# Two decoder layers with 32 routed experts on one core: fewer expert pairs scattered through DRAM, read back inside the expert stage, and a new router chain

## What is computed

```python
x = x + concat(rglru, conformer_conv, retention)(rmsnorm(x) @ w_in) @ w_out
x = x + hier_moe(rmsnorm(x), ...)

def hier_moe(x, wg, bg, we, be, w1, w3, w2):
    pg = softmax(x @ wg + bg); g = argmax(pg)              # 1 of 4 groups
    top_v, top_i = top_k((x @ we + be)[group g], 2)        # 2 of its 8 experts
    gates = pg[g] * softmax(top_v)
    y = sum over the 32 experts e: gates_e * (silu(x @ w1_e) * (x @ w3_e)) @ w2_e
```

## Time and profile before

| | us |
|---|---|
| median of three runs | 904.78 |
| profiled execution, its own time | 911.48 |
| its span, first to last instruction | 909.2 |
| TensorE busy (4940 matmul records) | 795.3 |
| VectorE busy | 352.5 |
| ScalarE busy | 169.7 |
| GpSimd busy | 119.1 |
| moved by DMA | 266.57 MB |

### The profile page before, as it was taken

One profiled execution on the slowest core, in us unless ns is written; L12 is line 12 of the kernel. 1 busy time (PEld: TensorE's weight loads), 2 busy tenths in 40 slices (PEclk: granted clock), 3 DMA queues, 4 the chain that ended last, 5 costly groups with the idle time before them and its releaser, 6 DMA issues.

```text
span 909.2 us, 12840 instructions
## 1 busy us (share of the span) xinstructions
PE 795.3 (87%) x4940; PEld 469.6 (52%) x4940; DVE 352.5 (39%) x865; ACT 169.7 (19%) x357; POOL 119.1 (13%) x163
## 2 busy tenths in 40 slices
PE   7999999979998887887789999999899987788784
PEld 6745554765554444454277446447655534445451
DVE  2468986532111111111722789955311211111127
ACT  2304113101211111111211121221011111111113
POOL 0101030030111010011000000300211101011010
PEclk9999999989999999999979999999999999999997
DMA  9961933879999999997983038348799999999961
GB/s 291 306 243 60 317 98 88 279 220 353 419 416 416 414 416 414 416 416 275 340 267 138 1 125 245 97 122 321 233 392 415 415 418 415 416 416 416 392 232 53
DMA packets 107918, 266.57 MB, mean 293 GB/s; under 512 B 34775, under 2 KB 68587, under 8 KB 90902
## 3 DMA queue, kind: packets, MB, share of 16 engines
q1 hardware_dynamic: 97898, 254.11, 75.2%
q0 software_dynamic: 8640, 9.11, 2.9%
q10 hardware_dynamic: 1340, 2.80, 0.8%
HBM read 262.85 MB, written 25.92 MB: 318 GB/s over the span
## 4 chain that ended last, share of the span: by engine, by line
PE 52%; DMA 24%; issue 12%; DVE 6%; SPq 3%; ACT 1%; POOL 1%; DVEq 0%; POOLq 0%; ACTq 0%
DMA ring<-in_moe_w 22%; PE psum L1008 13%; PE psum L723 12%; PE psum L1034 9%; PE psum L702 7%; PE psum L654 3%; PE psum L734 2%; SPq L509 1%; DVE arena L1649 1%; DMA rows<-xn_scratch,sg 1%; PE psum L892 1%; PE psum L660 1%; SPq L505 1%; SPq L501 1%; PE psum L790 1%
## 5 line engine op out<-in xcount | busy, mean ns | idle before, releaser
L1008 PE MATMUL psum<-ring,arena 128*64 128x256 f32 x1984 | 229.2, 383 | 36.1 <-DVE arena L1649 26.0
L1008 PEld LDWEIGHTS psum<-ring,arena 128*64 128x64 f32 x1984 | 148.5, 137 | 102.2 <-issue 38.5
L1034 PE MATMUL psum<-ring,arena 128*64 128x512 f32 x496 | 124.9, 633 | 39.3 <-DMA ring<-in_moe_w 31.2
L1657 DVE SCALAR_TENSOR_TENSOR arena<-arena,psum 128x128 f32<-128x128 f32 x64 | 18.1, 282 | 298.7 <-ACT arena L1945 283.1
L723 PE MATMUL psum<-ring,uT 128*128 128x512 f32 x256 | 113.0, 595 | 0.0
L1034 PEld LDWEIGHTS psum<-ring,arena 128*64 128x64 f32 x496 | 40.3, 144 | 107.5 <-issue 106.2
L1649 DVE TENSOR_TENSOR arena<-psum,gff 128x512 f32<-128x512 f32 x64 | 41.2, 685 | 118.9 <-PE psum L654 118.9
L2063 POOL DMA_INDIRECT y_scratch<-arena,sg x28 | 28.3, 1010 | 374.8 <-ACT arena L1930 314.0
L723 PEld LDWEIGHTS psum<-ring,uT 128*128 128x128 f32 x256 | 47.7, 190 | 55.3 <-issue 54.5
L1935 ACT ACTIVATE arena<-psum 128x256 f32<-128x256 f32 x62 | 23.8, 384 | 280.1 <-PE psum L1008 270.8
L1930 ACT ACTIVATE arena<-psum,sg 128x512 f32<-128x512 f32 x64 | 44.0, 687 | 129.3 <-PE psum L1034 129.3
(11 more groups left out here) (285 smaller groups left out, 656.0 us busy)
## 6 DMA issues: line engine op xcount, KB each, us to landing
ring<-in_moe_w SPq DMA_DIRECT2D x186, 1024.0 KB
ring<-in_w_in SPq DMA_DIRECT2D x24, 1024.0 KB
ring<-in_w_out SPq DMA_DIRECT2D x8, 1024.0 KB
y_scratch<-sg SPq DMA_DIRECT2D x2, 2304.0 KB
ring<-y_scratch SPq DMA_DIRECT2D x4, 1024.0 KB, 9.8
arena<-in_state_ret SPq DMA_DIRECT2D x16, 128.0 KB, 6.2
out<-arena SPq DMA_DIRECT2D x16, 128.0 KB, 2.6
xn_scratch<-rows ACTq DMA_DIRECT2D x4, 512.0 KB, 4.6
```

The source lines that it names most:

```text
L1008: i = pe.matmul(b[64 * j:64 * j + 64, 0:FE], xsT[:, u // 2, k, s], w[j][:, k, :], start=k == 0, stop=k == KT - 1, skip_group_check=True)
L1034: i = pe.matmul(b[64 * q:64 * q + 64, :], hT[:, q, f, :], w[:, 512 * j:512 * j + 512], start=f == 0, stop=f == 1, skip_group_check=True)
```

## The change

- **Way back.** Pairs 0 to 9 go through DRAM (`VIA_DRAM` = 10), pairs 10 to 15 by matmul. Each pair has its own sums now: five parts (`back0` to `back4`) that take turns in banks 6 and 7, each added to `x` by VectorE before the next may use the bank. GpSimd reads the rows of pairs 0 to 9 back by an indirect gather per tile and choice (`read_back`, two DMAs a tile, tiles in the order 1, 2, 0), issued at its turns 10, 11 and 12 behind the wait for the results of that pair; VectorE adds them (`sums`) at its turns 12, 13 and 14. A row that is not in `y_scratch` is skipped by the DMA, so VectorE clears both landing tiles first (`clear`).
- **No zeros.** `y_scratch` is filled once, from `w_out`, in the first layer's mixer, and never zeroed.
- **Spare.** It is expert 30 now, not 31; its w2 is loaded between the weights of the pairs (at SP's turn 4).
- **Input weights.** SP issues granules 6, 7, 0, 1, 8, 3, 4, 2, 5 of the next `w_in` right behind the last expert's w2, each when its granule is free, and 9 to 11 after the extra loop.
- **Router.** TensorE transposes raw `x`; the logits come out token by row and VectorE applies 1/rms and bias in one step; ScalarE scales and stores the rows. Slots are one-hot marks of the rank in the expert, made on VectorE; a first table gives the tokens (`tab`) and starts the gathers, a second the gates (`tabg`), a third the overflow (`tabo`), whose marks (`overs`) VectorE makes after the first tokens. `keep_clock` has 11, 5, 5 and 4 matmuls in place of 17, 26 and 17.
- **Turn.** `up` waits for x0 alone and for x1 half way; `tokens` is cut in two around `up` of the second expert.

```diff
-VIA_DRAM = NPAIR - 2
+VIA_DRAM = 10
+BY_MATMUL = NPAIR - VIA_DRAM
+READ_BACK = (1, 2, 0)
-WAIT_NORM, WAIT_CHOICE, WAIT_MARKS, WAIT_ROWS = (13, 8), 17, 26, 17
+WAIT_NORM, WAIT_CHOICE, WAIT_MARKS, WAIT_GATES, WAIT_ROWS = (13, 8), 11, 5, 5, 4
 # SP
-                sp.dma_start(y_dram.rearrange("(p r) (h n) -> p (r h) n", p=64, h=2),
-                             bc(sg[0:64, 2:3, :], [64, 2 * 9, 512])).then_inc(y_zeroed, 16)
+                    if p == 4:
+                        sp.wait_ge(idx_ready, l + 1)
+                        for f in range(2):
+                            sp.dma_start(spare_w2[f], w2[l, NE - 2, 128 * f:128 * f + 128, :]).then_inc(spare2_in, 16)
-                sp.wait_ge(scattered, 16 * VIA_DRAM * (l + 1))
-                for t, (o, n) in enumerate(TILES):
-                    sp.dma_start(ring[0:n, 9 + t, :] ...).then_inc(sums_in[t], 16)
+                if l + 1 < DEPTH:
+                    for g, use in zip((6, 7, 0, 1, 8, 3, 4, 2, 5), last_use):
+                        xfull(sp, *use, l)
+                        project_in(l + 1, g)
 # TensorE
+                def experts2_back(p):
+                    pair, it = pair_of(p)
+                    up(2 * pair, it, spare=p == NPAIR - 1)
+                    if p - 2 >= VIA_DRAM:
+                        give_back(p - 2, (2, 3))
+                        give_back(p - 2, (4,))
+                    down(1 - pair, it if pair else it - 1)
+                    turn_h(2 * pair, it)
+                    if p + 1 < NPAIR:
+                        tokens(pair + 1, it, (0,))
+                    up(2 * pair + 1, it)
+                    if p + 1 < NPAIR:
+                        tokens(pair + 1, it, (1,))
+                    turn_h(2 * pair + 1, it)
+                    if p - 1 >= VIA_DRAM:
+                        give_back(p - 1, (0, 1))
 # VectorE
+                def clear():
+                    own(dve.memset(again[0], 0.0))
+                    own(dve.memset(again[1], 0.0))
+                    own.wait()
+                    dve.sem_inc(again_clear, 1)
+                def experts2_back(p):
+                    pair, it = pair_of(p)
+                    if p - 2 >= VIA_DRAM:
+                        given_back(p - 2, (0, 1))
+                        if p - 2 - VIA_DRAM < 3:
+                            sums(p, READ_BACK[p - 2 - VIA_DRAM])
+                            if p - 2 - VIA_DRAM < 2:
+                                clear()
+                        given_back(p - 2, (2, 3, 4))
+                    if p - 1 >= VIA_DRAM:
+                        rest(p - 1, 0)
+                    hidden(2 * pair, it)
+                    if p - 1 >= VIA_DRAM:
+                        rest(p - 1, 1)
+                        low(p - 1)
+                    if p + 1 < NPAIR:
+                        tokens(pair + 1, it)
+                    hidden(2 * pair + 1, it)
 # GpSimd
+                def read_back(t):
+                    o, n = TILES[t]
+                    pool.wait_ge(again_ready, l + 1)
+                    pool.wait_ge(scattered, 16 * VIA_DRAM * (l + 1))
+                    pool.wait_ge(again_clear, 3 * l + READ_BACK.index(t) + 1)
+                    for k in range(2):
+                        pool.indirect_dma_start(out=again[k][0:n, :], out_offset=None, in_=y_dram, ...)
...
                     if g < VIA_DRAM:
                         scatter(g)
                     else:
-                        way_back(g - VIA_DRAM)
+                        way_back(g)
                     if g + 2 < NPAIR:
+                        if g >= VIA_DRAM:
+                            for j in range(2):
+                                xfreed(pool, f"y{j}", *pair_of(g), l)
                         gate_of(g + 2)
+                    if 0 <= g - VIA_DRAM < 3:
+                        read_back(READ_BACK[g - VIA_DRAM])
```

More of the change, by code:

```diff
@@ L415, in expert_job @@
             pair, e = 2 * it + u, 4 * it + u
-            b, n = {"x0": (0, pair), "x1": (1, pair), "h": (2, e), "hT": (3, e), "y0": (4, pair), "y1": (5, pair)}[kind]
+            back = 2 * it + u - VIA_DRAM
+            b, n = {"x0": (0, pair), "x1": (1, pair), "h": (2, e), "hT": (3, e), "y0": (4, pair), "y1": (5, pair),
+                    "back0": (6, 3 * back), "back1": (7, 2 * back), "back2": (6, 3 * back + 1), "back3": (7, 2 * back + 1),
+                    "back4": (6, 3 * back + 2)}[kind]
             return b, l * PER_BANK[b] + EXPERT_BASE[b] + n
[L419 to L429, removed]
         def xfull(eng, kind, u, it, l):
@@ L1031, in down @@
                                 w = ring[:, 6 * pair + 3 * q + 2, 1024 * f:1024 * f + 1024]
-                                if spare and q:
+                                if spare and not q:
                                     w = spare_w2[f]
@@ L1066, in experts2 @@
-                def experts2(pair, it, first=False):
+                    if 4 in parts:
+                        b = begin("back4", pair, it)
+                        for n_, y in enumerate((y_top, y_mid, y_low)):
+                            for q in range(4):
+                                i = pe.matmul(b[32 * q:32 * q + 32, 0:256], back[:, pair, SEQ:NT], y[:, 256 * q:256 * q + 256],
+                                              start=n_ == 0, stop=n_ == 2, skip_group_check=True)
+                        finish(i, "back4", pair)
+                        return
@@ L1082, in _ @@
                     experts2(1, it)
[L1083 to L1091 removed]
+                for p in range(VIA_DRAM, NPAIR):
+                    experts2_back(p)
+                give_back(NPAIR - 2, (2, 3))
@@ L1624, in _ @@
-                by_pair = tab[:, :, 0:NE].rearrange("p v (g i) -> p v g i", i=2)
-                for i in range(2):
-                    h = slice(64 * i, 64 * i + 64)
-                    own(dve.tensor_copy(sel[h, :, 0:NPAIR], by_pair[h, :, :, i]))
-                free(dve.tensor_copy(sel[:, :, NPAIR:], tab[:, :, NE:NBLK]), "tab")
-                freed(dve, l, "tab")
-                own.wait()
-                do(S(selu[:, :], sel[:, 0, :], float(OUTSIDE), None, ALU.add))
-                S(gidx[:, :], selu[:, :], 1, None, ALU.logical_shift_right).then_inc(idx_ready, 1)
@@ new lines, in _, with token_of @@
+                dve.wait_ge(gidx_ready, l + 1)
+                def token_of(a, b):
+                    do(dve.tensor_copy(tok[:, 0, a:b], gidx[:, a:b]))
+                    for t in (1, 2):
+                        own(S(tok[:, t, a:b], tok[:, 0, a:b], float(-128 * t), None, ALU.add))
+                    own.wait()
+                token_of(0, NPAIR)
+                dve.sem_inc(tok_ready, 1)
+                full(dve, l, "tabg")
+                free(dve.tensor_copy(sel[:, 0:NPAIR], bank("tabg")[:, 0:NPAIR]), "tabg")
@@ new lines, in overs_marked @@
+                def overs_marked():
+                    full(dve, l, "tabo")
+                    own(dve.memset(gidx[64:128, NPAIR:], OUTSIDE))
+                    own(dve.memset(sel[64:128, NPAIR:], 0.0))
+                    own(S(gidx[0:64, NPAIR:], bank("tabo")[0:64, 0:OVER], float(OUTSIDE), None, ALU.add))
+                    free(dve.tensor_copy(sel[0:64, NPAIR:], bank("tabo")[0:64, OVER:2 * OVER]), "tabo")
+                    freed(dve, l, "tabo")
+                    own.wait()
+                    token_of(NPAIR, NPAIR + OVER)
+                    dve.sem_inc(idx_ready, 1)
```

557 lines of the change are left out of this document (307 added, 250 removed).

## The result

The changed kernel takes **942.12 us** (median; 939.70 to 946.68), the kernel before beside it 904.45 (903.02 to 905.32): a ratio of **1.0425**, with an interval of 1.0384 to 1.0467. The forecast was slower, 912.8, with a range up to 922. The sign was right; the loss is 37.7 us and not 8, and the time lies 20 us above the range. The profiled execution took 939.7, of which 937.7 is its span.

A forecast was written before the change was run, and what follows sets the result against it. The weight stream bounds the expert stage; elsewhere TensorE and chains between engines count. Router, spare, way back and end sum to +1.9 in layer 0 and +6.1 in layer 1: 904.8 + 8.0 = 912.8 us, range 895 to 922.

The forecast's parts named there:

- a ring: Expert stage, turns 12 to 14: one `down` waits through read-back, additions, `clear` and part 4: 21.9, 20.8, 17.7 us.
- +11.2 a layer: Turns 12 to 14: the three laps sum to 60.4 us against 49.2 before; bounds 0 to +17.
- the landing: Turns 12 to 14: the read-back's second gather lands after 9.1, 8 and 7 us.
- `down` to issue: Turns 12 to 14: from `down` start until GpSimd can issue the read-back, gate copy included, 5.6 us.
- rival B: Turns 12 to 14: waits lower the clock, a slow `down` adds 1.7 us; up to +10, 922 us; chance 0.09.
- +17: Upper bound a layer for turns 12 to 14: landings of 10.3 us each and `down` at 5.35 instead of 3.65.
- Rival A: Turns 12 to 14: read-back lands before it is asked for, only bytes count, +2.3 a layer; 895.0 us; chance 0.25.
- -12.3: Router, layer 0: earlier indices, gather and first `up` save 12.3 us; in layer 1 the saving is 8.1.
- The 2.8 us for the zeros: Router, layer 0: the first gather no longer falls beside the zeroing of `y_scratch`, 2.8 us saved.
- The spare: Weight stream: the spare expert's w2, 1.05 MB, now loaded inside it, costs +2.7 us a layer.
- The end: Expert stage, turn 15 and after: +0.8, +1.5 and -2.0, in sum +0.3 us a layer.
- I take the difference over as it is: Final step: the profiled execution stands 6.7 us over the median, and the forecast keeps that difference.

The follow-up runs named there:

- the second profile of the kernel before: The kernel before, unaltered, run again for a second profiled execution: median 906.22 us, the profiled execution 908.24 us.
- its own run: The spare expert's w2 not loaded, against the order alone: 897.09 us, ratio 0.9904 against the kernel before.
- the order alone: Changed kernel with VectorE adding back2 to back4 ahead of `sums` and `clear`: 902.61 us, ratio 0.9973 against the kernel before.
- the second comparison: The changed kernel run again, unaltered, beside the kernel before: 940.44 us, ratio 1.0369.
- The early issue: Changed kernel with GpSimd issuing `read_back` ahead of the wait for the pair's results, VectorE's order kept: 902.66 us, ratio 0.9948 against the kernel before.

## Where the prediction was right, and why it came out far too low

**The mechanism: right.** There is a ring from `down` through read-back, additions, `clear` and part 4 to the next `down`, and it is the term that decides. The chain shows each of its steps, cutting it at either of two places removes some 38 us, and lengthening it by 2.3 us twice a layer costs 10.0.

**Its size: the step that failed.** +11.2 a layer was +20.3 and +20.9, 18.8 us too little in both layers. By the lap's table +9.2 in layer 0: 5.0 of it are the slow `down`s and what follows them to the issue, 1.4 the issue (I counted one gather of 1.04 and a gap; a read-back's gather and its gap are 1.6 to 1.7), 1.8 the landing, 1.0 the rest. In layer 1 the landing is the largest with 3.6, then the `down`s with 3.0. So two terms of the sum were mis-sized above all: `down` to issue, put at 5.6 and measured at 5.4 to 7.8, and the landing, put at 9.1, 8 and 7 and measured at 10.5 to 11.4, 6.3 to 6.7 and 9.1 to 9.7.

I had the slow `down` as rival B, at 0.09, with a price of 1.7 each. For turns 13 and 14 it was no rival but a consequence of the forecast itself: a ring that makes TensorE idle 4 to 8 us a turn also lowers its clock, and fillers in the wait took 6.8 us off. (The `down` that opens turn 12 comes ahead of the ring's first wait; it took 5.24 in layer 0 and 3.65 in layer 1.) The earlier trace rows showed a `down` of 5.35 behind 2.86 us of idle time; I should have taken that row for the later laps. The price of 1.7 was near (1.6 to 2.4 in layer 0), and it comes on top of the landing, not instead of it.

**The range.** My upper bound for the three laps, +17, doesn't follow from its own terms. Landings of 10.3 make 23.1, 23.1 and 21.0, three slow `down`s add 5.1: 72.3 against 49.2, **+23.1**. The measured +20.3 and +20.9 lie inside that. Taken in both layers it gives 936.6. The range ended at 922, below even the 924.4 that the +17 as I wrote it would give.

**The landing.** 9.1 was near for 128 rows (10.53, 11.35 in layer 1); what I took off for the last turn (7) and for the 32 rows (8) was wrong both ways: 9.06 and 6.31. I had taken 2 us off in turn 14 because the stream's backlog would be partly gone. It was not: over that landing DMA moved 394 GB/s, against 412 over turn 12's:

```profile
364.20:374.70 10.50, 8.30 (x60) 4.37 (x56) 2.96 (x6) 1.04 (x3) 3.52 (x5) 1.00 1.01 412
...
411.90:421.00 9.10, 8.28 (x60) 4.34 (x56) 2.95 (x6) 1.04 (x3) 3.52 (x5) 1.00 1.01 394
```

Why it took 9.06 and not 10.53 stays open. No read-back ran beside an idle queue. The estimate from the Trainium skill, "DMA: Bandwidth & Descriptors", section "Anatomy of one DMA — SWDGE (gpsimd) path" (3.5 us) doesn't hold here: the trace has six landings of 6.3 to 11.4 us beside the weight stream. Rival A, which it spoke for, did not come.

**The router.** -12.3 was -8.8, -8.1 was -6.6. In layer 0 the indices are out at 182.73, not 181.5, because the table takes its upper end; VectorE's row waits for nothing else, and TensorE's rows are

```profile
179.24 3.07 PE L973 MATMUL psum<-v 128*64 128x16 f32 x24
...
189.54 1.91 PE L654 MATMUL psum<-const,rows 128*128 128x128 f32 x8
191.69 3.67 PE L1032 MATMUL psum<-ring,arena 128*64 128x256 f32 x32 [0.23 <-DVE arena L1739]
```

24 records of 16 columns at 0.13 each, as much as 128 columns took the earlier trace rows: I had let the price fall with the columns. (The weight loads of the gates' table, of the same shape, take 2.96 us for 24, so it may be the loads that set the price; no run tests it.) The tokens' transposes took 1.91 where the earlier trace rows has 1.16. Over 150 to 205 us the granted clock is 0.88 and was 0.94, so a part of both may be the clock; no run separates that.

The gather itself came as forecast: issued at 183.65, it landed 4.2 us later, at 187.9. But TensorE was not there to take it. Its program has the gates' table (L973 again) and the last fillers (L660) ahead of the tokens' transposes, and the fillers had begun 0.2 us before the rows landed (GpSimd's timeline, the view of the DMAs issued from 183 to 184.5 us, TensorE's timeline):

```profile
183.65 1.20 POOL L2184 DMA_INDIRECT rows<-xn_scratch,sg  x1 [45.58 <-DVE sg L1652]
...
rows<-xn_scratch,sg POOLq DMA_INDIRECT x1, 4.2
...
184.68 3.07 PE L973 MATMUL psum<-v 128*64 128x16 f32 x24
187.68 2.08 PE L660 MATMUL psum<-const 128*128 128x128 f32 x8
```

The transposes start at 189.54, 1.7 us after the landing, and 1.7 in layer 1 (649.36, with a landing of 4.3 behind an issue at 643.35). I had written that the gates are no longer ahead, and had put this at nothing. It is the largest part of the 3.5 us that are missing in layer 0; the late indices are 1.2 and the transposes 0.75. In layer 1, 1.7 of the -6.6 are not the router's: the next mixer's first 64 products took 17.48 in the profile of before, and 15.79 in that of after and in the second one of before. The 2.8 us for the zeros I had costed from one row of one execution: the second profile of the kernel before has that gather at 5.59 with the same zeros. `up` at full speed, 1.4, came as forecast.

**The spare.** Right as a price (5.5 for two layers by its own run), though between the two profiles it shows as -0.5 and +1.3: the profile of before ran 2.2 us slower in that very stretch than its second one. Router and spare together: forecast -15.0, measured -14.6 in the spans. The errors all but cancel.

**The end.** +0.6 forecast, +1.9 measured. Turn 15 is 18.8 and 18.3, not 16.4: its `down` runs 6.31 and 5.81 behind the last lap. Without the read-back it is 16.16, with the order alone 17.5 and 17.2. No additions from DRAM stand behind the last `down`.

**From one execution to the median.** The terms above make 20.5 of the 29.3 us that the forecast was too low. The other 9 are the step "I take the difference over as it is": the profile of before stood 6.7 above its median, that of after 2.4 below its own. The second profile of before stands only 2.0 above its median (906.22). Its distance to the profile of after is 31.5, and the medians of the second comparison lie 32.5 apart, those of the first 37.7. The 5 us between the two comparisons I can't place.

**What would have been without the ring.** Rival A's sum was 895.0. With the ring cut the kernel takes 902.6, and even without a read-back 896.3. Between `down` of pairs 10 and 15 the order alone takes 81.2 in layer 0 and 82.3 in layer 1 against 76.7 and 76.4 before: turns of 16.7 to 17.7 and a last turn of 12.9 for 11.8. Of the turns 1.8 us in layer 0 are TensorE's waits for gathered rows, one of which landed 13.1 us after its issue (10.3 at most before). I had counted +2.6 a layer for this. Behind the last `down` 2 to 3 us come back. So router and read-back all but cancel, and the change without its ring gives half a per cent at most. The early issue has 0.9948 with an interval below 1, but its median, 902.66, is that of the order alone (902.61, 0.9973 with 1 inside), so the two are not told apart.

## What to carry to other kernels

When a buffer that returns by a long way (DRAM, a queue, another engine) is consumed in the same in-order program as a short hand-over, write down who waits for whom from one repeat to the next: if the path closes, its length replaces the pace of the stage, and one change of order on one engine opens it. Price such a ring with the slow form of each instruction in it, since the idle time that it makes also lowers TensorE's clock. And take the terms of a sum from more than one row where the same work appears more than once, and not from an execution that stands off its median.

## What the runs showed of the hardware

The clock fell within a single wait: over 8 us of idle time the granted clock went to 0.50, and the `down` behind it took 6.04 for 3.65. With fillers of no use in most of that wait the same `down` took 5.35, and the next one 3.65 where it was 5.2 to 5.4; so matmuls without a purpose bought 6.8 us. A `down` behind 2.7 to 2.9 us of waiting was slow in one place and fast in another (5.24 and 3.65, both ahead of the ring).

An indirect gather costs by its rows too: the two gathers over a tile of 128 landed 12.2 us after the first issue, one alone 9.1; over a tile of 32 it was 7.9 and 6.5. In the router, away from the weight stream, the first gather landed in 4.2. Products with 16 moving columns took 0.13 a record, about as much as those with 128 (0.12). A memset of 128x1024 float32 took 0.91, and the next one could start 1.07 after it.
